# Gate and up projections of a feed-forward block computed by a seven-product block scheme, on one Trainium2 core

## The reference, cut to what matters

```python
def _swiglu(h, w_gu, w_down):
    g, u = jnp.split(h @ w_gu, 2, axis=-1)
    return (jax.nn.silu(g) * u) @ w_down

for i in range(DEPTH):
...
    h = _rmsnorm(x, norm_ffn_g[i])
    x = x + _swiglu(h, ffn_w_gu[i], ffn_w_down[i])
```

## Time and profile before

| | us |
|---|---|
| median of 3 runs | 1846.71 (1844.95 to 1848.64) |
| the profiled execution, as timed | 1846.44 |
| its span in the trace | 1844.9 |
| first feed-forward part, first gate matmul to the next wait | 387.09 to 926.96 |
| second feed-forward part, the same | 1287.76 to 1831.31 |

### The profile page before, as it was taken

The page is one execution under the profiler, slowest core; times in us unless marked ns, Lnnn a source line. Parts: engine busy times, 40 slices in busy tenths (PEclk is TensorE's granted clock), DMA queues, the critical chain, the costliest instruction groups (busy, mean ns, idle before and its releaser), DMA issues.

```text
span 1844.9 us, 26151 instructions
## 1 busy us (share of the span) xinstructions
PE 1815.8 (98%) x10714; PEld 1777.1 (96%) x10714; DVE 627.9 (34%) x912; ACT 502.4 (27%) x737; POOL 427.1 (23%) x489
## 2 busy tenths in 40 slices
PE   7999999999999999999999999999999999999998
PEld 7999888989999999999999999999999999999998
DVE  6142564352231222212351367434312221222224
ACT  5222555132211111111132247632311111111111
POOL 4000121662110211011560033345321011200224
PEclk9999999999999999999999999999999999999999
DMA  5310011412212221121232101141122211222111
GB/s 187 108 51 23 24 46 58 152 46 69 68 52 67 68 68 59 55 69 51 63 115 68 47 24 35 35 160 63 53 68 68 69 55 59 68 69 67 42 52 69
DMA packets 108512, 123.20 MB, mean 67 GB/s; under 512 B 4336, under 2 KB 104752, under 8 KB 108176
## 3 DMA queue, kind: packets, MB, share of 16 engines
q1 hardware_dynamic: 107376, 122.00, 20.1%
q10 hardware_dynamic: 1056, 0.07, 0.0%
HBM read 112.62 MB, written 9.44 MB: 66 GB/s over the span
## 4 chain that ended last, share of the span: by engine, by line
PE 94%; DVE 2%; ACT 1%; DMA 1%; issue 0%; POOL 0%; SPq 0%; DVEq 0%; ACTq 0%; POOLq 0%
PE bank L383 93%; DVE ht L1399 1%; DVE w_lo L1381 1%; DMA raw<-in_mlstm_w_out_dram 0%; ACT w_hi L969 0%; DVE w_lo L1387 0%; POOL h_lo L1928 0%; DMA xs<-in_x_prompt_dram 0%; ACT w_hi L976 0%; PE bank L957 0%; PE bank L601 0%; PE bank L450 0%; PE bank L729 0%; ACT h_hi L993 0%; ACT rstd L1001 0%
## 5 line engine op out<-in xcount | busy, mean ns | idle before, releaser
L383 PE MATMUL bank<-h_hi,w_hi 128*128 128x384 f32 x1920 | 654.2, 341 | 4.6 <-DVE w_lo L1387 1.8
L383 PE MATMUL bank<-h_lo,w_hi 128*128 128x384 f32 x1920 | 647.3, 337 | 0.0
L383 PE MATMUL bank<-h_hi,w_lo 128*128 128x384 f32 x1920 | 646.9, 337 | 0.0
L1381 DVE TENSOR_TENSOR w_lo<-raw,w_hi 128x2048 fp32r<-128x2048 f32 x91 | 220.6, 2424 | 476.1 <-ACT w_hi L969 476.1
L383 PEld LDWEIGHTS bank<-h_hi,w_hi 128*128 128x128 f32 x1920 | 360.9, 188 | 16.4 <-POOL h_lo L1928 5.7
L383 PEld LDWEIGHTS bank<-h_lo,w_hi 128*128 128x128 f32 x1920 | 361.1, 188 | 1.2 <-issue 0.2
L383 PEld LDWEIGHTS bank<-h_hi,w_lo 128*128 128x128 f32 x1920 | 361.0, 188 | 0.6
L969 ACT CAST w_hi<-raw 128x2048 fp32r<-128x2048 f32 x91 | 173.6, 1908 | 649.1 <-PE bank L383 635.4
L383 PE MATMUL bank<-a_hi,w_hi 128*128 128x384 f32 x704 | 236.1, 335 | 0.0
L383 PE MATMUL bank<-a_hi,w_lo 128*128 128x384 f32 x704 | 235.8, 335 | 0.0
L383 PE MATMUL bank<-a_lo,w_hi 128*128 128x384 f32 x704 | 235.8, 335 | 0.0
(11 more groups left out here) (182 smaller groups left out, 1806.0 us busy)
## 6 DMA issues: line engine op xcount, KB each, us to landing
raw<-in_ffn_w_gu_dram SPq DMA_DIRECT2D x44, 1024.0 KB, 5.1
raw<-in_ffn_w_down_dram SPq DMA_DIRECT2D x16, 1024.0 KB, 5.2
raw<-in_gla_w_in_dram SPq DMA_DIRECT2D x12, 1024.0 KB, 5.3
raw<-in_mlstm_w_in_dram SPq DMA_DIRECT2D x11, 1024.0 KB, 5.3
x_keep<-xT SPq DMA_DIRECT2D x2, 3072.0 KB, 9.7
xT<-x_keep SPq DMA_DIRECT2D x8, 768.0 KB, 6.6
raw<-in_ffn_w_down_dram SPq DMA_DIRECT2D x8, 768.0 KB, 4.6
raw<-in_mlstm_w_out_dram SPq DMA_DIRECT2D x4, 1024.0 KB, 7.5
```

The source lines that it names most:

```text
L383: return nc.tensor.matmul(out, lhsT, rhs, start=start, stop=stop)
L1381: V.tensor_tensor(w_lo[s][:, :, :], raw[s][:, :, :], w_hi[s][:, :, :].bitcast(F32), ALU.subtract).then_inc(w_lo_ready, 1)
```

## The change

The gate and up projections, except for the first pair of each layer, use Strassen's scheme in Winograd's form. A tile is a 2 x 2 block product: two column chunks by two K halves of 4 chunks on the weight side, two K halves by two token halves on the other. Eight block products of 4 chunks become seven, with sums of blocks before and after.

- `BLOCKS` becomes (4, 2, 4, 4, 4, 4): six blocks in a layer, so twelve pairs of down projection over 4 or 2 chunks for six over 8 or 6. `a_hi` and `a_lo` move into `y_parts`.
- Weight side, per tile: DVE makes four sums of 128x512 out of `raw` (`fast_sums`, three of them, and one in `fast_low` after j = 0), ACT rounds seven operands of 128x512 (`fast_high`), and DVE takes their rests (`fast_low`). The seven operands ("units") fill `w_hi` and `w_lo` of both slots, so there is one set of them: unit j of the next tile is written when product j of this tile is done.
- Activation side, once a layer in `first_pair`: DVE makes four sums of 128x1536, then ACT and DVE split four operands of that size (`t_high`, `t_low`). For this the normed x now goes into `qkv` instead of the ring `ht`.
- Result side, per tile: ACT copies product 0 out of its bank, DVE makes seven additions of 128x384 with one operand in a bank (`fast_pair`). Products 4, 5 and 6 of a tile reuse the banks of 0, 1 and 2, after DVE has read them. Silu now works in place on `sg`, and DVE multiplies `at` by `sg`, both in SBUF (`times`).
- In the last block ACT squares x and POOL only adds; the PE, ACT, DVE and POOL loops over pairs are written out.

```diff
-BLOCKS = (8, 8, 6)
-PAIRS = 25
+BLOCKS = (4, 2, 4, 4, 4, 4)
+PAIRS = 8 + sum(BLOCKS) // 2 + 2 * len(BLOCKS)
...
+ORDER = (0, 3, 1, 2)
+SEEN = tuple(ORDER.index(g) + 1 for g in range(4))
...
+            def fast_tile(q, s, sp, L=None):
+                u = 2 * sp + s
+                def product(j, b, r_hi, r_lo):
+                    out = bank[4 * s + b][:, 0:HT]
+                    for k in range(4):
+                        at_w = 2 * (j % 4) + k // 2, slice(k % 2 * P, (k % 2 + 1) * P)
+                        w = w_hi[j // 4][:, at_w[0], at_w[1]]
+                        mm(out, w, r_hi[:, k, :], k == 0, False)
+                        mm(out, w, r_lo[:, k, :], False, False)
+                        last = mm(out, w_lo[j // 4][:, at_w[0], at_w[1]], r_hi[:, k, :], False, k == 3)
+                    return last
...
+                pe.wait_ge(taken[s], 4 * q)
+                pe.wait_ge(op_lo, 6 * u + 1)
+                product(0, 0, *h_parts(0, 0)).then_inc(p_done, 1)
...
+                pe.wait_ge(op_lo, 6 * u + 4)
+                product(3, 3, *h_parts(1, 0)).then_inc(p_done, 1)
...
+                pe.wait_ge(op_lo, 6 * u + 5)
+                pe.wait_ge(c_read, 6 * u + 1)
+                product(4, 0, *t_parts(1)).then_inc(p_done, 1)
...
+                pe.wait_ge(w_lo_ready, 2 * q + s + 1)
+                pe.wait_ge(c_read, 6 * u + 2)
+                product(6, 2, *h_parts(1, 1)).then_inc(mm_done[s], 4)
...
-                            pe.wait_ge(a_ready, f0 + 4 * (k // 2) + 2 * half + k % 2 + 1)
+                            pe.wait_ge(a_ready, f0 + 4 * (k // 2) + SEEN[2 * half + k % 2])
...
+            def fast_high(q, s, u, j, after_plain=False):
+                if j == 0:
+                    act.wait_ge(raw_loaded[s], 16 * (q + 1))
+                if after_plain:
+                    act.wait_ge(mm_done[j // 4], 4 * q)
+                elif j < 6:
+                    act.wait_ge(p_done, 6 * (u - 1) + j + 1)
+                else:
+                    act.wait_ge(mm_done[1 - s], 4 * q + 4 * s)
+                if j == 1:
+                    act.wait_ge(op_sum, 4 * u + 3)
...
+                nc.scalar.copy(unit(w_hi, j), w_source(s, j)).then_inc(op_hi if j < 6 else w_hi_ready, 1)
...
+            def fast_sums(q, s, u, e=None):
...
+                V.tensor_tensor(s_tmp[:, 0, :, :], w_block(s, 0, 0), w_block(s, 1, 0), ALU.subtract).then_inc(op_sum, 1)
+                dve.wait_ge(op_sum, 4 * u + 1)
+                V.tensor_tensor(w_block(s, 1, 0), w_block(s, 1, 0), w_block(s, 1, 1), ALU.add).then_inc(op_sum, 1)
+                dve.wait_ge(op_sum, 4 * u + 2)
+                V.tensor_tensor(s_tmp[:, 1, :, :], w_block(s, 1, 0), w_block(s, 0, 0), ALU.subtract).then_inc(op_sum, 1)
+            def fast_low(q, s, u, j):
...
+                V.tensor_tensor(unit(w_lo, j), w_source(s, j), unit(w_hi, j).bitcast(F32), ALU.subtract
+                                ).then_inc(op_lo if j < 6 else w_lo_ready, 1)
+                if j == 0:
...
+                    V.tensor_tensor(w_block(s, 0, 0), w_block(s, 0, 1), s_tmp[:, 1, :, :], ALU.subtract
+                                    ).then_inc(op_sum, 1)
+            def fast_pair(q, sp, f, nb):
...
+                    if not plain:
+                        fast_sums(nq, ns, u + 1)
+                        fast_low(nq, ns, u + 1, 0)
+                    dve.wait_ge(p_done, 6 * u + 2)
...
+                    V.tensor_tensor(u1, p1, out[1], ALU.add).then_inc(c_read, 1)
+                    if not plain:
+                        fast_low(nq, ns, u + 1, 1)
+                    dve.wait_ge(p_done, 6 * u + 3)
+                    dve.wait_ge(c_read, 6 * u + 1)
+                    V.tensor_tensor(u2, u1, out[2], ALU.add).then_inc(c_read, 1)
...
+                    V.tensor_tensor(dst[:, 2, :], v, out[2], ALU.add).then_inc(taken[s], 4)
...
+            def first_pair(L, q, f, e):
...
+                times(0)
+                dve.wait_ge(lo_ready, NORM_S[e] + 16)
+                b11, b12, b21, b22 = h_block(0, 0), h_block(0, 1), h_block(1, 0), h_block(1, 1)
+                V.tensor_tensor(b11, b12, b11, ALU.subtract).then_inc(t_sum, 1)
...
+                t_low(L, 2, 1)
+                t_low(L, 3, 2)
+                t_low(L, 1, 3)
+                fast_sums(q + 1, 0, u, e)
+                times(2)
+                for j in range(4):
+                    fast_low(q + 1, 0, u, j)
+                times(3)
+                fast_low(q + 1, 0, u, 4)
+                t_low(L, 4, 4)
+                fast_low(q + 1, 0, u, 5)
+                fast_low(q + 1, 0, u, 6)
```

More of the change, by code:

```diff
@@ L905, in _ @@
                                     tile_group(1, gs[1], h_of, KC)
[L906 to L907 removed]
                         for s in range(2):
[L909 removed]
+                            fast_tile(q + 1, s, 10 * L, L)
+                        start = 2
+                    for i in range(start, n_pairs):
+                        for s in range(2):
+                            fast_tile(i + q0 + PGU[b], s, i + (10 * L + FAST[b]))
                     f0 = 4 * (FFP * L + sum(BLOCKS[:b]) // 2) + 4
@@ L963, in _, with split @@
         def _(act):
-            def split(q, s, wait=True):
+            def split(q, s, wait=True, nb=KC):
                 act.wait_ge(raw_loaded[s], 16 * (q + 1))
@@ new lines, in t_high, with first_pair @@
+            def t_high(L, n):
+                act.wait_ge(t_sum, 4 * L + (4 if n == 4 else 3))
+                dst = t_parts(n)[0].rearrange("p (h c) t -> p h c t", h=2)
+                nc.scalar.copy(dst, t_source(n)).then_inc(t_hi, 1)
+            def first_pair(L, q):
+                u = 20 * L
+                for g in range(4):
+                    act.wait_ge(taken[1], 4 * q + (g - 3))
+                    src = take(q, 0, g)
+                    nc.scalar.activation(sg[:, g, :], src, ACT.Silu).then_inc(taken[0], 1)
+                    if g == 1:
+                        for n in (2, 3, 1):
+                            t_high(L, n)
+                for j in range(5):
+                    fast_high(q + 1, 0, u, j, True)
+                act.wait_ge(mm_done[0], 4 * q + 4)
+                act.wait_ge(mm_done[1], 4 * q + 4)
+                t_high(L, 4)
+                fast_high(q + 1, 0, u, 5, True)
+                fast_high(q + 1, 0, u, 6, True)
@@ L1323, in _ @@
                 for b, nb in enumerate(BLOCKS):
-                    with act.Fori(0, nb // 2) as i:
-                        q = i + q0 + PGU[b]
-                        for g in range(4):
-                            act.wait_ge(taken[1], 4 * q + (g - 3))
-                            src = take(q, 0, g)
-                            nc.scalar.activation(sg[:, g, :], src, ACT.Silu).then_inc(taken[0], 1)
-                        split(q + 1, 0)
-                        split(q + 1, 1)
+                    n_pairs = nb // 2
+                    if b == 0:
+                        first_pair(L, q0 + PGU[0])
+                    for i in range(1 if b == 0 else 0, n_pairs):
+                        fast_pair(i + q0 + PGU[b], i + 10 * L + FAST[b], nb if i == n_pairs - 1 else None)
                     if L == 0 and b == 0:
@@ L1849, in pair @@
                         add_residual(q, 0, g, c + g % 2)
-                    split(q + 1, 0)
+                    if fast is None:
+                        split(q + 1, 0, nb)
+                    else:
+                        fast_sums(q + 1, 0, fast)
+                        for j in range(4):
+                            fast_low(q + 1, 0, fast, j)
                     if back:
@@ L1854, in pair @@
                         add_residual(q, 1, g, c + (2 + g % 2))
-                    split(q + 1, 1)
+                    if fast is None:
+                        split(q + 1, 1, nb)
+                    else:
+                        for j in range(4, 7):
+                            fast_low(q + 1, 0, fast, j)
                 pair(q0 + POUT, 0, True)
```

307 lines of the change are left out of this document (255 added, 52 removed).

## The result

The median goes from 1846.86 us (1844.95 to 1848.64, 4 runs) to 1819.19 us (1818.20 to 1821.50, 4 runs): ratio 0.985, 95% interval 0.9835 to 0.9869, so 27.7 us faster. The forecast was 1771.5 us with a range to 1800; the gain is a third of the 83.3 us that the removed matmuls are worth. The profiled execution took 1819.81 us.

The account below looks back on a forecast made before the run. PE, running matmuls at its own pace, was taken as the bound. 1846.44 - 83.3 (matmuls) + 5.4 (entries) - 2 (ring) + 3 (two-chunk blocks) + 2 (other block ends) = 1771.5 us, range 1758 to 1800.

Parts of the forecast that it names:

- Removed matmuls: Gate and up tiles after each layer's first pair: 480 fewer matmuls at 0.1736 us, 83.3 us off the path.
- Costed at nothing: Matmuls of the new products: same 0.1736 us step as before, and new PE waits, two a product, add nothing.
- The steady pair: Changed pairs: DVE needs 22.5 us plus 3 beside POOL, 25.5 of PE's 29.2, so no steady loss.
- B: Rival: DVE bounds the steady pair, 30.1 us against PE's 29.2, 18 us over 20 pairs, 1790 us; chance 0.11.
- The rule it went with: Steady pair on DVE: next operation waits until the pipe has emptied, so every operation costs its full duration.
- D: Rival: slower than before, DVE and POOL take turns at SBUF, 34.7 us a pair, 1881 us; chance 0.05.
- The entry: First changed tile of each layer: `u1` late for product 4, stall 2.7 us a layer, 5.4 together.
- cover of 0.6 us for the first rest: Layer entry: DVE's first rest ends at 420.3, PE arrives at 420.9, so it just fits.
- The term of 2 us for the dropped ring of the norm: Layer entry: DVE's norm no longer follows POOL, `w_lo` for slot 1 comes earlier, 1 us gained a layer.
- Block ends: Last gate and up results before down tiles: 1.5 us for each two-chunk block, 0.2 for each of ten others.
- Rival C: At 12 block ends PE stands for `raw`, sums and first rest, 3 us each, 36 us, 1807; chance 0.10.
- A: Whole kernel: the forecast itself, own range from its bounds 1758 to 1785 us; chance 0.74.

Follow-up runs that it names:

- mend2: Changed kernel with reordered layer entry, first down tile's column chunks side by side, casts ahead of Silu, next layer's rest behind two last additions; 1791.73 us.
- casts: Changed kernel with ACT's casts of operands 3 to 6 put ahead of the Silu beside them in gate tiles; 1819.18 us.
- load3: Changed kernel with three of each changed tile's seven rests made twice on DVE; 1851.00 us.
- frag: Kernel before with only the activations cut into the changed kernel's six blocks, full products kept; 1858.82 us.
- side: Changed kernel with the first down tile of a pair running its two column chunks side by side; 1810.65 us.
- lastadd: Changed kernel with DVE's rest for the next layer moved behind two of the last additions at the end of layer 1; 1819.01 us.
- filler: Changed kernel with useless matmuls, 38 ahead of product 0 and 16 ahead of product 4, in each layer's first changed tile; 1817.60 us.
- place: `frag` with the rounded activations and their rests moved into y_parts, as in the changed kernel; 1862.64 us.

## Why the prediction was right or wrong

**Removed matmuls: right.** 480 fewer, and an unbroken run in `mend2` of 0.1744 us each. "Costed at nothing" for the new operands was off by 0.9 ns a matmul, 5 us in all: I took the step of one stretch of gate and up tiles for products whose operands lie elsewhere; that the place is the reason is shown for down tiles only.

**The steady pair: right.** Forecast 22.5 us of DVE and 3 for POOL; the window has 24.32 busy, 84% of the pair where 25.5 of 29.2, 87%, was put with POOL's share. Starts of 128x512 operations that wait for nothing are 0.60 apart, 0.72 behind their source, as put. `u1` came at 6.6, not 5.9, due at 8.3. One thing was not seen: the 1.10 us for ACT's cast, which `casts` shows to be free. B is refuted: there is no PE wait in a steady pair. But `load3` shows how near it was: 4.3 us more a pair, and PE waits in every block. The rule it went with, from the Trainium skill, "VectorE: DVE Perf Modes", section "The DRAIN you can't avoid", has an exception in the same paragraph, which the prediction left out: an operation that is not held starts earlier. The rows at 643.35, 643.95 and 644.42 (0.60 and 0.47 apart for 0.69 and 0.55 of duration) agree with the exception. D fell with B, since POOL is met by few operations, though each meeting is dear, as D had it (the row at 695.62).

**The entry: wrong, the step "the first pair starts at 387.09 and has 192 matmuls, so it ends near 420.9".** It is the largest error, 20 us of 48. The piece of 3104 matmuls in the earlier trace rows starts at 387.09 because the chain comes to PE there, over DVE's `w_lo`. PE's own first 48 matmuls of that pair had by then been run, beside POOL's `h_lo`, as this window of the kernel before shows:

```profile
376.50:387.08 10.58, 9.79 (x48) 8.07 (x48) 8.61 (x7) 4.38 (x6) 10.58 (x8) 1.00 0.01 2
```

So 144 of the 192 were left, which take 25.0 us, and some 2 more because a part of them is paced by `h_lo` again: the pair ends near 414.1 before, and in the changed kernel, whose opening is 2.1 us later, at 416.1. The forecast had 420.9 (and 387.09 + 192 x 0.1736 is 420.4, so its cover of 0.6 us for the first rest was 0.1 by its own numbers). DVE came nearly as forecast at first, with the same 2.1 added: sums from 406.5 for 404.4, first rest ended at 423.0 for 420.3. `u1` ended at 436.3 for 432, so 2.2 later than that: several operations of 128x512 took 1.31 to 1.37 us beside POOL's split of `at`. Where 0.6 us of cover were counted for the first rest, PE was 6.9 us ahead of it, and the order of DVE's queue (the next tile's sums ahead of `u1`) did the rest. Of the 20 us, PE's early arrival is 2 x 6.9, DVE's later `u1` 2 x 2.2, and the next term 2. The chain of waits shows where the *chain* enters an engine, not where that engine began its work.

The term of 2 us for the dropped ring of the norm was worth nothing: L1732 takes 8.14 us for 8 as L1399 did, and PE still waits 0.71 us for `w_lo` at 389.15, 0.72 before.

**Block ends: right in kind, a factor of four too small.** 5 us forecast, 18.9 found. The prediction followed the last result of a four-chunk block, which fits, as it said. It did not follow the third, which is needed 1.6 us into the down tile. It had followed both only for the two-chunk blocks, where the sum was 1.5 and PE waits 1.13 + 1.48 in layer 1 and 1.12 + 0.61 in layer 2, and then 1.6 more for `u1`, which had no term. It also took 0.5 for a product `at` by `sg` that takes 1.38 beside POOL (row at 695.62), having named that very slowing, and left out the weight rest ahead of the third result in DVE's queue, 0.6 us.

Rival C (3 us at each of 12 block ends, 1807) had the nearest mechanism and the nearest number of all, but not its cause: no PE wait there is for `raw` or sums except after the two-chunk block.

**Before the next layer: not in the sum.** 3.0 us, because the run of matmuls in the earlier trace rows goes through it without a wait, and I looked no further: a long rest stands in front of the last additions, and the shorter last block leaves no time to catch up. `frag` has waits at the same two places, 7.5 us, with POOL making the squares too, so it is not the same chain.

**Low clock and the opening: not in the sum.** 1.5 us are the clock behind product 4 in layer 1. The opening of 2.1 us lies ahead of the feed-forward work, and in large part it is the clock near 300 us (below): chance, and no error of the reasoning. Some 3 us in the two parts stay unexplained.

**The range** held A with its bounds and B. The bounds of the entry (0 to 5 us a layer) were made from DVE's side only; PE's arrival had no bound, being taken as a reading.

## What to carry to other kernels

Before you put work on an engine at the seam between two phases, take the start of each engine's work from its own timeline, not from the piece in the chain of waits, and ask of every result when the *first* reader wants it, not only when the last one does. Where an engine's queue is full, change the order before you take work away: here the order alone gave 14 us at the two entries, as much as leaving the work out. A waiting list is a bound on what a repair can give only where no other engine sets the time behind it.

## What the hardware showed beyond that

**The clock after a stall.** PE's granted clock goes to its lower level (1.2 of 2.4 GHz) for a few microseconds in this kernel: 6.8 us at 420.3, as PE stands, 3.4 at 437.3 behind the wait of 2.89, 3.4 at 918.6 behind the wait of 2.45; matmuls are then 0.32 us apart. Before, none such appears ahead of the tail. Not each such wait has it: product 4 of layer 2 waits 2.11 us at 1325.60 and goes on at full clock. The 2.7 us wait near 300 us, which all kernels have, is followed by low clock in eleven of the fourteen traces, and not in the kernel before's, `side`'s and `lastadd`'s, though `side` and `lastadd` have the changed kernel's code up to there. From that wait to the first feed-forward matmul it is 76.2 to 76.4 us in these three and 77.5 to 78.1 in the others: 1.1 to 1.9 us by chance of an execution, as far as one trace of each kernel can say, and so part of the 2.1 us of the opening. `filler` shows that it costs time only where PE sets the pace.

**DVE beside POOL.** A DVE operation with both inputs in SBUF takes 0.56 us alone and 1.38 beside POOL (128x384), 0.69 and 1.37 (128x512); POOL's 128x384 goes from 1.00 to 1.26 and 2.37. DVE operations with one input in a bank keep 0.55. That agrees with the Trainium skill, "GPSIMD Engine Reference", section "Specifications", by which the two share SBUF interfaces and get in each other's way when DVE has two SBUF inputs; the durations are this case's.

**The place of an operand.** 1.17 ns a matmul of 384 columns between the two places of `a` (`frag` and `place`). It is small; if it is also what makes the new products slower (0.94 ns a matmul in `mend2`), it is 5 us in this kernel.
